# Attention with per-head values, split halves side by side, two passes over two query blocks

## The reference

```
logits = einsum('bqhc,bqkc->bqhk', qb, c_sel) * HEAD_DIM ** -0.5
logits = where(valid, logits + bias, -inf)
p = softmax(logits)
o_lat = einsum('bqhk,bqkc->bqhc', p, c_sel)                   # 8 heads x 128 latents
attn_out = einsum('bshc,chd->bshd', o_lat, w_uv)              # 8 heads x 64
mix = concatenate([pool_out, attn_out]) @ w_o
```

## Time and profile before

| | us |
|---|---|
| three runs: median (lowest to highest) | 1267.05 (1266.28 to 1267.63) |
| profiled execution, its own time | 1263.58 |
| its span, first to last instruction | 1261.8 |
| busy in the span: PE, DVE, ACT, POOL | 1208.7, 833.4, 557.7, 512.5 |

### The profile page before, as it was taken

How to read it: one execution, slowest core, us unless ns; L and a number is a source line. 1 busy time by engine, 2 the same in 40 slices (tenths; PEclk the granted TensorE clock), 3 DMA queues, 4 the chain that set the end, 5 groups by cost and what they waited for, 6 DMA issues and landing times.

```text
span 1261.8 us, 16530 instructions
## 1 busy us (share of the span) xinstructions
PE 1208.7 (96%) x5761; PEld 979.6 (78%) x5761; DVE 833.4 (66%) x1201; ACT 557.7 (44%) x943; POOL 512.5 (41%) x370
## 2 busy tenths in 40 slices
PE   5999997989999999999999999989899999999997
PEld 3776785778788778788788789978788888888886
DVE  6388989557857888888988766647534233243357
ACT  4546542775165234244243366652342442433440
POOL 2235798424435676775865752202102102103002
PEclk9999999899999999999999999999999999999999
DMA  7723431101314333243242200024132333423331
GB/s 221 250 76 106 145 100 52 66 1 34 101 34 134 100 101 117 84 133 100 84 132 90 94 1 2 1 101 134 63 100 88 105 101 95 117 84 99 116 102 66
DMA packets 126564, 117.59 MB, mean 93 GB/s; under 512 B 5741, under 2 KB 99498, under 8 KB 126506
## 3 DMA queue, kind: packets, MB, share of 16 engines
q1 hardware_dynamic: 126506, 116.81, 30.4%
HBM read 106.29 MB, written 10.50 MB: 93 GB/s over the span
## 4 chain that ended last, share of the span: by engine, by line
PE 84%; DVE 6%; POOL 5%; ACT 2%; issue 2%; DMA 1%; POOLq 0%; DVEq 0%; ACTq 0%
PE g_bank L1540 16%; PE g_bank L1542 16%; PE g_bank L1541 16%; PE wide L1540 9%; PE wide L1542 9%; PE wide L1541 9%; PE g_bank L1500 4%; POOL wlo L417 2%; PE wide L1645 1%; DVE win L588 1%; PE wide L1604 1%; PE wide L1605 1%; PE g_bank L1692 1%; POOL rows L805 1%; POOL rstd L745 1%
## 5 line engine op out<-in xcount | busy, mean ns | idle before, releaser
L417 POOL TENSOR_TENSOR wlo<-wring,whi 128x1024 fp32r<-128x1024 f32 (+1 forms) x94 | 229.6, 2444 | 226.0 <-ACT whi L1413 121.7
L1540 PE MATMUL g_bank<-xhi,whi 128*128 128x512 f32 (+2 forms) x768 | 300.7, 392 | 4.8 <-DVE xlo L654 3.8
L1542 PE MATMUL g_bank<-xhi,wlo 128*128 128x512 f32 (+2 forms) x768 | 296.9, 387 | 0.0
L1541 PE MATMUL g_bank<-xlo,whi 128*128 128x512 f32 (+2 forms) x768 | 296.8, 386 | 0.0
L1413 ACT ACTIVATE whi<-wring 128x1024 fp32r<-128x1024 f32 x120 | 127.1, 1059 | 355.8 <-PE wide L1542 179.8
L417 DVE TENSOR_TENSOR wlo<-wring,whi 128x1024 fp32r<-128x1024 f32 (+1 forms) x66 | 84.4, 1279 | 197.6 <-ACT whi L1413 192.7
L1540 PE MATMUL wide<-whi,hhi 128*128 128x512 f32 x480 | 190.2, 396 | 0.7 <-POOL wlo L417 0.7
L1542 PE MATMUL wide<-whi,hlo 128*128 128x512 f32 x480 | 189.6, 395 | 0.0
L1541 PE MATMUL wide<-wlo,hhi 128*128 128x512 f32 x480 | 189.6, 395 | 0.0
L1540 PEld LDWEIGHTS g_bank<-xhi,whi 128*128 128x128 f32 (+1 forms) x768 | 143.8, 187 | 39.9 <-DVE xlo L654 4.3
L1541 PEld LDWEIGHTS g_bank<-xlo,whi 128*128 128x128 f32 (+1 forms) x768 | 143.9, 187 | 33.0 <-issue 1.8
(11 more groups left out here) (215 smaller groups left out, 1993.4 us busy)
## 6 DMA issues: line engine op xcount, KB each, us to landing
wring<-in_w_up SPq DMA_DIRECT2D x64, 512.0 KB, 4.0
wring<-in_w_down SPq DMA_DIRECT2D x64, 512.0 KB, 3.7
wring<-in_w_in SPq DMA_DIRECT2D x26, 512.0 KB, 3.9
wring<-in_w_o SPq DMA_DIRECT2D x16, 512.0 KB, 4.6
rows<-in_x SPq DMA_DIRECT2D x8, 512.0 KB, 5.0
normalized_rows<-rows SPq DMA_DIRECT2D x8, 512.0 KB, 6.9
rows<-normalized_rows SPq DMA_DIRECT2D x4, 512.0 KB, 5.2
emb_stage<-normalized_rows SPq DMA_DIRECT2D x4, 512.0 KB, 4.8
```

The source lines that it names most:

```text
L417: eng.tensor_tensor(parts_of(name, lo_tile(name)), parts_of(name, wring[n % 4]), parts_of(name, hi_tile(name)).bitcast(F32), ALU.subtract) ...
L1540: nc.tensor.matmul(out_ap, w_hi, m_hi, start=first, stop=False)
L1541: nc.tensor.matmul(out_ap, w_hi, m_lo, start=False, stop=False)
L1542: return nc.tensor.matmul(out_ap, w_lo, m_hi, start=False, stop=last)
```

## The change

- `block_head`: steps now alternate between two neighbouring blocks, with the same head: m % 2 picks the block, and one values product `pv` takes one head and two blocks (256 columns). It goes over the key blocks of the later block; the transposed probabilities of the earlier one are zero there, set by 8 memsets per chunk on POOL.
- Values: `values(c, k)` makes latents of block k times `w_uv` in three passes of 512 columns (8 heads x 64), 4 of them in chunk 0, 6 in chunk 1. ACT and DVE write `hi` and `lo` of each head side by side, 64 + 64 columns. That is the stationary operand `v_both`; probabilities' `hi` and `lo` move over it in two passes per key block. The result has the product with v_hi in 64 partitions and that with v_lo in the other 64; ACT copies one half (`other_half`) and DVE `fold` adds it to the other, straight into the transposed `att_outT`.
- `uv`, its copies and `aT` are gone. Row sums are inverted for four steps at a time (`reciprocals`), POOL spreads them over 64 columns (`spread_reciprocals`), PE transposes them (`rT`), and DVE `scale_heads` multiplies.
- Latent queries of chunk 1: two ahead of attention, six in steps 32 to 42.
- `lat_hi`, `lat_lo` are gone; `w_uv` is split once (ACT, then POOL). The first half of `latT` is split before chunk 0 (`latents_lo(0)`).
- Tiles are laid out anew. One values tile lies in `whi[1]`, so `wo` unit (1, 0, 1) is split after the last `pv`; others lie over `gains`, which are loaded a second time for chunk 1, on SP after the last `pv` and ahead of the last four `wo` units.

The diff, cut:

```diff
-        if c:
-            names += [("ql", 1, h) for h in range(HEADS)]
+        names += [("ql", 1, 0), ("ql", 1, 1)] if c else []
+        names += [("vv", c, k) for k in ((0, 1, 2, 3), (2, 3, 4, 5))[c]]
...
+def block_head(m):
+
+    c, r = divmod(m, 32)
+    pair, r = divmod(r, 2 * HEADS)
+    return CB * c + 2 * pair + r % 2, r // 2
+
+
 def attention_step(c, step):
 
     lo, hi = 32 * c, 32 * c + 32
     out = []
+    if c and step - lo in range(0, 12, 2):
+        out += [("ql", 1, (step - lo) // 2 + 2)]
+    if c and step - lo in (5, 9):
+        out += [("vv", 1, 6 + (step - lo) // 9)]
     if step % 2 == 1 and lo <= step - 3 < hi:
         out += [("pv", (step - 3) // 2)]
-    uv = [("uv", (step - 4) // 2)] if step % 2 == 0 and lo <= step - 4 < hi else []
-    transposes = []
     if step < hi:
-        i = step // HEADS
-        transposes = [("tr", step, t) for t in range((i + 4) // 4)]
-
-    out += uv + transposes if c else transposes + uv
-    if step % HEADS == 4 and lo <= step - 12 < hi:
-        out += [("aT", (step - 12) // HEADS)]
+        out += [("tr", step, t) for t in range((block_head(step)[0] + 4) // 4)]
+    if step % 4 == 2 and lo <= step - 6 < hi:
+        out += [("rT", (step - 6) // 4)]
...
+            sp.wait_ge(g_full, EV[("pv", 31)])
+            load_gains(ln1_g, ln1_b)
...
+            def spread_reciprocals(w):
+
+                if w >= 2:
+                    pool.wait_ge(rec_full, w - 1)
+                if w == 8:
+
+                    pool.wait_ge(g_evac, EV[("ql", 1, 3)])
+                pool.wait_ge(rec_ready, w + 1)
+                pool.tensor_copy(rec_rows(w).rearrange("p (e h d) -> p e h d", e=2, h=2),
+                                 exp_rec[:, w % 2, :].rearrange("p (h e) -> p e h", h=2).unsqueeze(3).to_broadcast([P, 2, 2, HD]))\
+                    .then_inc(rec_spread, 1)
...
+                for v in range(2):
+                    for k in (CB * c + 1, CB * c + 3):
+                        for tiles in (probs_hi, probs_lo):
+                            pool.memset(pair_slot(tiles, 16 * c + v)[:, k, 0, :].bitcast(F32), 0.0).then_inc(cells_zero, 1)
...
+                    if m % 4 == 3 and m - 7 >= 32 * c:
+                        spread_reciprocals((m - 7) // 4)
+                spread_reciprocals(8 * c + 7)
...
-            lo(("wo", 1, 0, 0), ("wo", 1, 0, 1))
+            lo(("wo", 1, 0, 0))
             head_masks(1)
-            lo(("wo", 1, 0, 2), ("wo", 1, 0, 3))
+            lo(("wo", 1, 0, 1), ("wo", 1, 0, 2), ("wo", 1, 0, 3))
...
+            def latents_lo(c):
+
+                at = slice(0, CHUNK * (c + 1))
+                dve.wait_ge(latT_hi_ready, c + 1)
+                nc.vector.tensor_tensor(latT_lo[:, at], latT[:, at], latT_hi[:, at].bitcast(F32), ALU.subtract)\
                     .then_inc(latT_lo_ready, 1)
...
+
+            def latent_query_lo(h):
+
+                name = ("ql", 1, h)
+                dve.wait_ge(g_evac, EV[name])
+                nc.vector.scalar_tensor_tensor(out=qlat_lo[:, h, :], in0=bank(name)[:, :], scalar=HD ** -0.5,
+                                               in1=qlat_hi[:, h, :].bitcast(F32), op0=ALU.mult, op1=ALU.subtract)\
+                    .then_inc(qlat_lo_ready, 1)
+
+            def values_lo(c, k):
+
+                name = ("vv", c, k)
+                dve.wait_ge(g_evac, EV[name])
+                v = v_pairs(k)
+                nc.vector.tensor_tensor(v[:, :, 1:3, :], bank(name)[:, :].rearrange("p (a e d) -> p a e d", a=4, e=2),
+                                        v[:, :, 0:4:3, :].bitcast(F32), ALU.subtract).then_inc(v_lo_ready, 1)
+
+            def fold(v):
+
+                name = ("pv", v)
+                main, _ = halves(v)
+                dve.wait_ge(g_evac, EV[name])
+                nc.vector.tensor_tensor(att_outT[main, v // 2 % 4, pair_tokens(v)], bank(name)[main, 0:2 * P], other_half(v)[main, :],
+                                        ALU.add).then_inc(folded, 1)
+
+            def reciprocals(w):
+
+                dve.wait_ge(exp_ready, 4 * w + 4)
+                nc.vector.reciprocal(exp_rec[:, w % 2, :], exp_sum[:, w % 2, :]).then_inc(rec_ready, 1)
+
+            def scale_heads(w):
+
+                dve.wait_ge(rec_full, w + 1)
+                dve.wait_ge(folded, 2 * w + 2)
+                a = att_outT[:, w % 4, pair_tokens(2 * w)]
+                nc.vector.tensor_tensor(a, a, bank(("rT", w))[:, 0:2 * P], ALU.mult).then_inc(heads_normed, 1)
 
             def attention(c):
                 for step in range(32 * c, 32 * c + 32 + 5):
                     if step < 32 * c + 32:
                         mask_logits(step)
+                    if step == 32 * c:
+                        for k in ((0, 1, 2, 3), (2, 3, 4, 5))[c]:
+                            values_lo(c, k)
+                    for name in attention_step(c, step - 1) if step > 32 * c else ():
+                        if name[0] == "ql":
+                            latent_query_lo(name[2])
+                        elif name[0] == "vv":
+                            values_lo(1, name[2])
                     if 32 * c + 2 <= step < 32 * c + 34:
                         probabilities_lo(step - 2)
-                    if step % HEADS == 3 and step - 11 >= 32 * c:
-                        scale_heads((step - 11) // HEADS)
+                    if step % 2 == 0 and 32 * c <= step - 4 < 32 * c + 32:
+                        fold((step - 4) // 2)
+                    if step % 4 == 1 and 32 * c <= step - 5 < 32 * c + 32:
+                        reciprocals((step - 5) // 4)
+                    if step % 4 == 3 and 32 * c <= step - 7 < 32 * c + 32:
+                        scale_heads((step - 7) // 4)
...
+            latents_lo(0)
...
+            latents_lo(1)
+            latent_query_lo(0)
+            latent_query_lo(1)
...
+                for k in ((0, 1, 2, 3), (2, 3, 4, 5))[c]:
+                    values_hi(c, k)
...
+                            v = name[1]
+                            main, other = halves(v)
+                            if v >= 4:
+
+                                act.wait_ge(folded, v - 3)
+                            copy_out(name, other_half(v)[main, :], ps[other, 0:2 * P])
+                        elif name[0] == "ql":
+                            latent_queries(1, [name[2]])
+                        elif name[0] == "vv":
+                            values_hi(1, name[2])
                     if step == hi:
                         mix_hi(c, 0)
+                    if c and step == hi + 1:
+                        hi_of(("wo", 1, 0, 1))
...
+            def values(c, k):
+
+                name = ("vv", c, k)
+                at = slice(k * P, k * P + P)
+                pe.wait_ge(wuv_lo_ready, 1)
+                pe.wait_ge(latT_lo_ready, c + 1)
+                free(name)
+                three_passes(bank(name)[:, :], latT_hi[:, at], latT_lo[:, at], wuv_hi[:, :], wuv_lo[:, :], True, True)\
+                    .then_inc(g_full, 1)
+
             def logits(m):
-                i, h = divmod(m, HEADS)
+                i, h = block_head(m)
+                if m >= 32:
+                    pe.wait_ge(qlat_lo_ready, h + 1)
...
+                if c == 0:
+                    evacuated(("ql", c, 7))
+                    pe.wait_ge(relu_ready, 16)
+                else:
+
+                    pe.wait_ge(relu_ready, 48)
+                    pe.wait_ge(latT_lo_ready, 2)
                 logits(lo)
                 logits(lo + 1)
+                for k in ((0, 1, 2, 3), (2, 3, 4, 5))[c]:
+                    values(c, k)
+                pe.wait_ge(cells_zero, 8 * c + 8)
...
+                            i, h = block_head(2 * v + 1)
+                            pe.wait_ge(probs_lo_ready, TR[("tr", 2 * v + 1, (i + 4) // 4 - 1)])
+                            pe.wait_ge(v_lo_ready, VALUES[("vv", c, (3, 5)[c] if i < 6 else 7)])
                             free(name)
                             for k in range(i + 1):
...
+                                v_both = v_pairs(k)[:, h // 2, 2 * (h % 2):2 * (h % 2) + 2, :].rearrange("p b d -> p (b d)")
+                                for tiles in (probs_hi, probs_lo):
+                                    last = nc.tensor.matmul(bank(name)[:, 0:2 * P], v_both,
+                                                            pair_slot(tiles, v)[:, k, :, :].rearrange("p h q -> p (h q)"),
+                                                            start=k == 0 and tiles is probs_hi,
+                                                            stop=k == i and tiles is probs_lo)
                             last.then_inc(g_full, 1)
-                        elif name[0] == "uv":
-                            v = name[1]
-                            evacuated(("pv", v))
+                        elif name[0] == "rT":
+                            w = name[1]
+                            pe.wait_ge(rec_spread, w + 1)
                             free(name)
```

(13 more changed lines are left out.)

160 lines of the change are left out of this document (77 added, 83 removed).

## The result

The changed kernel takes 1278.76 us (median of 4 runs, 1278.26 to 1283.69) against 1266.91 for the kernel before, run beside it (4 runs, 1266.28 to 1267.63): a ratio of 1.0102 with a 95% interval of 1.0076 to 1.0128. It is slower, as forecast, but by 11.9 us where the forecast had 4.4; 1271.5 was predicted. The two profiled executions differ by more than the medians, 1278.30 against 1263.58: 14.7 us.

What follows compares the result with a forecast made beforehand. TensorE's column work bounds the attention stages now; DVE's queue order would become the bound. +2.2 us in each chunk gave +4.4 on 1263.58: 1268.0, plus 3.5 to the median: 1271.5 us, range 1255 to 1279.

Steps and rivals of the forecast that it cites:

- the term for masks 33 to 45: Chunk 1's attention: DVE's waits for query copies and folds make its order the bound; 31.0 to 43.6 us, +12.6.
- such a spell: Start of chunk 1's attention: TensorE idles 3 us and its clock falls to half; +1.5 us, between 0 and 5.
- (a): Odd steps 33 to 43: DVE waits 1.54 us for ACT's query copy before the remainder, with `probabilities_lo` queued behind.
- The start of chunk 1: Mask 32 waits for GpSimd, then value copies and remainders come before mask 33, at 735.8; +2.5 us.
- Mask 1 of chunk 0: Start of chunk 0's attention: mask 1 stands behind the values' copies and remainders, from 225.01 to 231.8; +6.8 us.
- The savings: Masks 45 to 63 -10.8 us, chunk 1's tail -3.6, masks 17 to 31 -2.6, chunk 0's tail -2.4.
- The MLP stages are the same: Outside the attention stages: the MLP stages neither gain nor lose time, 0 us.
- TensorE as the bound throughout: Rival: TensorE stays the bound, so its saved work shortens the kernel; -14 us, 1253; 22%, most of the way included.
- The lasting half clock: Rival: half clock lasts through chunk 1's queries, TensorE needing about 10 us a pair; +17 us, 1288; 6%.
- The shorter chain: Rival: DVE's chain in masks 33 to 45 is about half as long, about +7 us; 1266; 22% with cheaper starts.
- the cheaper starts: Rival: mask 1 of chunk 0 and mask 33 together come 5 us earlier; 1266; 22% with the shorter chain.
- The rule weighed: `latents_lo(0)`, two SBUF inputs, is shut out by GpSimd instructions reading SBUF, not by writing ones; mask 0 up to 0.5 us later.

Runs made afterwards that it cites:

- e3: Changed kernel plus unread transposes that keep TensorE busy in the tail of chunk 0's attention; 1278.94 us, ratio 1.0113 to the kernel before.
- e2: Changed kernel with the probabilities' second parts put ahead of the query's and late values' remainders on DVE; 1266.22 us, ratio 1.0004 to the kernel before.
- e1: Changed kernel with all eight latent queries of chunk 1 made ahead of its attention again; 1261.7 us, ratio 0.9969 to the kernel before.
- e5: Changed kernel with the edits of e1, e2 and e4 together; 1259.51 us, ratio 0.9945 to the kernel before.
- e4: Changed kernel with zero fills behind each chunk's first two masks and ACT's value copies ahead of the first exponentials; 1275.05 us, ratio 1.0075.
- e7: e5 with the four value remainders of each chunk's start behind mask 1 (33) in place of ahead; 1258.31 us, ratio 0.9947 to the kernel before.
- e6: e5 with the projection's first remainders ahead of the last fold on DVE in both tails; 1252.5 us, ratio 0.9892 to the kernel before.
- e8: e6 with GpSimd's second part of the first output weight piece moved behind mask 33; 1252.44 us, ratio 0.9892 to the kernel before.
- e9: e6 plus 52 unread transposes on TensorE ahead of the last pooling product; 1250.46 us, ratio 0.9871 to the kernel before.
- e11: e9 with the value remainders behind mask 1 (33), as in e7; 1249.56 us, ratio 0.9871 to the kernel before.
- e10: Kernel before plus 52 unread transposes on TensorE ahead of the last pooling product; 1266.8 us, ratio 1.0000 to the kernel before.

## Why the prediction was right in sign and wrong in size

**The step that failed** is the term for masks 33 to 45: 43.6 us forecast and 48.6 measured, +17.6 for +12.6. What was wrong in it is the sentence "TensorE needs ... in sum 5.3, for the same pair. DVE's order becomes the bound." It added DVE's own waits and set TensorE beside them as a separate engine that is merely faster. What holds `probabilities_lo` up holds a bank, the bank holds the next transposes, and these stand in TensorE's order ahead of the logits and the product that DVE waits for next. The prediction named it ("queued behind it are `probabilities_lo`") and priced it only for `rT`. The six pairs from mask 33, forecast at 4.75, 6.64, 8.43, 7.68, 8.43 and 7.68, took 4.68, 9.18, 9.29, 8.10, 9.25 and 8.10. Of the 2.5 us that the second took over its forecast, 1.4 is a spell at half clock (the same pair takes 7.74 in e3, at full clock). The sum had +1.5 for such a spell, at the start of chunk 1. Without the spell the term is 3.6 us short.

The sign and most of the size are thus the mechanism that was forecast, DVE's wait for the query's copy. By the runs the 17.6 us are: 12.5 for the place of `probs_lo` behind the other remainders (changed kernel to e2; up to 2.3 of it for the two late value blocks, by e1 to e5), 5.9 for having the queries in these steps at all, their time on TensorE and the half clock (e2 to e5, which has e4's edits too), less 0.8 that e5 is shorter than before.

The profiled difference, 14.7, exceeds the 4.4 forecast by 10.3. This stretch gives 3.5 of it (+17.6 for +12.6 and +1.5), the two rows that the forecast put at nothing 4.1, the two tails 1.4, masks 1 to 31 1.2 and masks 45 to 63 0.7; the starts take back 0.7. So the stretch alone does not make the miss: the clock in the two rows put at nothing is as large.

**Terms that held.** (a): DVE idles 1.58 to 1.63 us ahead of each query's remainder (1.54 forecast). The start of chunk 1: +2.4 for +2.5, and e4 showed its two parts. Mask 1 of chunk 0: +6.2 for +6.8, but with luck in it. The same instructions up to there came to mask 1 at 231.20 (the changed kernel), 232.14 (e3), 232.27 (e1) and 234.63 (e2); from mask 0 to mask 1 they took 4.5 us in the first two, where the half clock was over by 226 and 227, and 6.6 and 6.8 in the others, where it lasted until 230 and 233. The changed kernel and e2 at the four value products (columns as in the earlier trace rows):
```profile
226.00:230.00 4.00, 3.11 (x15) 2.59 (x15) 2.49 (x6) 2.32 (x6) 1.81 (x3) 1.00 0.43 161
...
228.00:232.00 4.00, 3.96 (x9) 3.15 (x10) 1.23 (x4) 1.69 (x4) 0.94 (x2) 0.50 0.12 47
```
Masks 1 to 17 took 20.2, the forecast pair of 2.5 eight times, which is 20.0 and not the 19.4 of its sum. The savings: -10.1, -2.9, -2.2 and -1.7 for -10.8, -3.6, -2.6 and -2.4. In masks 45 to 63 the change pays what the pass count said, in every version (55.25 to 55.30 us), while both tails came 0.7 to 0.8 us longer than forecast, which no run traces to one instruction.

**Terms that were missing.** "The MLP stages are the same" was true of their work and not of their clock: +2.4 in chunk 0. In the changed kernel TensorE is idle 1.34, 1.44 and 1.80 us in that tail, and the projection then runs at 1.2 GHz until after 290. The idles have a share in it: the half clock lies over this projection in all six executions with that tail (the changed kernel, e1, e2, e4, e5, e7) and in none of the five in which the last idle is gone (e6, e8, e9, e11) or all are filled (e3). But they are not the whole cause: e10 has the tail of the kernel before, with no idle above 1.16 us, and fell there all the same (0.66 in 281.75 to 286.75, 443.51 us for the row). So a part of the +2.4 may be that the one execution of the kernel before kept its clock. The second spell, in the MLP of chunk 1, is a matter of chance as far as the traces go. The same instructions with the same idle, before:
```profile
892.85 0.28 PE L1542 MATMUL g_bank<-xhi,wlo 128*128 128x256 f32 x1
895.05 0.39 PE L1540 MATMUL g_bank<-xhi,whi 128*128 128x256 f32 x1 [1.92 <-DVE xlo L654]
895.27 0.28 PE L1541 MATMUL g_bank<-xlo,whi 128*128 128x256 f32 x1
```
and after:
```profile
906.04 0.28 PE L1659 MATMUL g_bank<-xhi,wlo 128*128 128x256 f32 x1
908.24 0.54 PE L1657 MATMUL g_bank<-xhi,whi 128*128 128x256 f32 x1 [1.92 <-DVE xlo L696]
908.57 0.42 PE L1658 MATMUL g_bank<-xlo,whi 128*128 128x256 f32 x1
```
One runs on at full speed, the other is at half speed for 3.5 us (granted 0.51 in 908.24 to 911.73): the +1.7 of the last row of the table.

**The offset** between profile and median, +3.5 in the forecast, was +0.5 for the changed kernel. It hid 2.9 us of the 14.7. It too is mostly the clock: the profiled execution of the kernel before, 1263.58, had a mean granted clock of 0.992, and of the 17 executions beside e1 to e4 the two at 0.992 took 1263.5 us, the five at 0.990 1266.3 to 1267.2 and the two at 0.987 and 0.988 1268.0 and 1268.1 (the four at 0.989, with 1265.5 to 1266.5, break the order). The 3.5 was no constant that could be added to another kernel.

**The rivals.** The first, TensorE as the bound throughout at 1253, was wrong for this kernel and near for its work: with edits of order and none of arithmetic (e6) it takes 1252.5. That the figures meet is partly luck, since the rival gave -14 and e6 is 10.5 below the kernel before by the profiled executions, 12.7 by the medians of its chip. It was to be decided by a pair under 5.6 us in steps 33 to 43: the changed kernel's take 8.1 to 9.3 after the first, and e5's masks 33 to 45 give 5.0 a pair. The lasting half clock (1288) did not come: 0.96 granted from mask 33 to mask 45. The shorter chain and the cheaper starts (both 1266) fell with the table.

**The rule weighed.** `latents_lo(0)` took 0.91 us in the changed kernel, where GpSimd's mask sum, which reads SBUF, began at 225.79, and 0.69 in e7, where the fills, which only write, lay beside it. It is 0.91 in all four traces with the sum beside it (the changed kernel, e1, e2, e3) and 0.69 in all seven with the fills (e4 to e9, e11):
```profile
225.88 0.91 DVE L1084 TENSOR_TENSOR latT_lo<-latT,latT_hi 128x512 fp32r<-128x512 f32 x1 [3.48 <-ACT latT_hi L1562]
```
```profile
226.65 0.69 DVE L1083 TENSOR_TENSOR latT_lo<-latT,latT_hi 128x512 fp32r<-128x512 f32 x1 [3.47 <-ACT latT_hi L1561]
```
By the Trainium skill (SBUF — State Buffer, "Who interferes with whom") two inputs in SBUF contend with a reading GpSimd and not with a writing one: the traces agree, at 0.2 us. That the one is shut out for the whole length of the other, as the prediction put it, they do not show: 0.36 us of the first sum was still to run, by GpSimd's spans, which are rough.

## What to carry to other kernels

Where engines pass buffers round in a ring, an instruction that waits costs what stands behind it, on its own engine and on every engine whose next buffer those instructions free: follow the chain through the ring before you call one engine "merely faster". Put what frees a buffer ahead of what waits for something fresh; here this alone was worth 12.5 us for no change in work. And a stage's saving is only seen once its order lets the bounding engine run through.

## What was not expected of the hardware

Filling one idle stretch of TensorE does not simply buy back its half clock. In e3, e9 and e10 the clock stayed full where the idle was filled and fell at a later idle that it had passed at full clock until then. The fills are not shown to be what moved it: e8, whose instructions are those of e6 all through chunk 0, fell at the same place with nothing filled. e6 and e8 there (columns as in the earlier trace rows):
```profile
350.00:356.00 6.00, 4.70 (x38) 4.46 (x38) 1.01 (x2) 1.08 (x2) 0.00 (x0) 1.00 0.01 3
...
350.00:356.00 6.00, 5.70 (x35) 5.70 (x36) 0.24 (x1) 0.00 (x0) 0.00 (x0) 0.72 0.02 3
```
Over all their executions the fills of e9 and e10 did raise the mean granted clock: 0.995 to 0.998 in e9 where e6 had 0.991 or 0.992, and 0.990 to 0.994 in e10 where the kernel before had 0.988 to 0.992 beside it. In e10 that bought no time.

Projection and MLP of chunk 0, the same work in every version, took 440.5 us in two executions (before, e6), 441.6 to 442.0 in four (e3, e8, e9, e11) and 442.9 to 443.5 in seven (the changed kernel, e1, e2, e4, e5, e7, e10). A single profile therefore carries 1 to 3 us that belong to the clock and not to the edit, and up to 3 more at the start of chunk 0. The Trainium skill (TensorE: Matmul & The Clock Gate, "A second HAM failure mode: psum-queue depth-cycling") tells of short idles between groups, from PSUM banks being passed round, that make the clock go up and down: this case does not bear it out. The changed kernel waits up to 1.6 us for a bank in each pair of steps 35 to 45, yet its clock fell once in them (0.89 in 745 to 760), and in e2 the bank waits are gone and the clock in that stretch is 0.88.
